# Convolution-branch layer norm: the reciprocal deviation computed with tokens on partitions and spread by diagonal products

## What is computed

```python
u_a = a_val * jax.nn.sigmoid(a_gate)
v_a, nb_a = _causal_dwconv(u_a, buf_a, conf_dw)          # width 31
v_a = v_a + conf_dw_b
y_a = silu(_layernorm(v_a, conf_ln_g, conf_ln_b)) @ conf_pw
# _layernorm: mu, var over the 512 channels of a token;
#   (x - mu) * rsqrt(var + EPS) * g + b
```

## Time and profile before

| | us |
|---|---|
| median of 3 runs | 876.55 |
| lowest, highest | 872.9, 877.35 |
| profiled execution, its time | 875.98 |
| profiled execution, its span | 874.2 |
| TensorE busy | 840.3 (96%) |
| VectorE busy | 683.9 (78%) |
| ScalarE busy | 465.0 (53%) |
| GpSimd busy | 74.3 (9%) |

### The profile page before, as it was taken

One profiled execution on the slowest core, in us unless ns is written; L12 is line 12 of the kernel. 1 busy time (PEld: TensorE's weight loads), 2 busy tenths in 40 slices (PEclk: granted clock), 3 DMA queues, 4 the chain that ended last, 5 costly groups with the idle time before them and its releaser, 6 DMA issues.

```text
span 874.2 us, 14904 instructions
## 1 busy us (share of the span) xinstructions
PE 840.3 (96%) x5047; PEld 698.9 (80%) x5047; DVE 683.9 (78%) x939; ACT 465.0 (53%) x556; POOL 74.3 (9%) x71
## 2 busy tenths in 40 slices
PE   7899999999999999999999989999999999999994
PEld 2489999989899999899777457888888888887841
DVE  0772637978797777599448889999899998999877
ACT  4642442343432221632222458888888888888741
POOL 0002000000000000230000010000000010005640
PEclk9999999999999999999999999999999999999988
DMA  9868534445544221123761579978997899999752
GB/s 332 276 191 289 189 118 160 129 161 169 168 127 122 91 79 49 55 78 119 238 246 73 187 280 397 399 282 333 352 368 249 316 400 400 400 397 400 294 195 98
DMA packets 90998, 201.24 MB, mean 230 GB/s; under 512 B 8793, under 2 KB 13401, under 8 KB 90919
## 3 DMA queue, kind: packets, MB, share of 16 engines
q1 hardware_dynamic: 78813, 165.25, 53.6%
q0 software_dynamic: 5136, 18.42, 6.0%
q10 hardware_dynamic: 7003, 16.95, 5.3%
HBM read 182.97 MB, written 18.35 MB: 230 GB/s over the span
## 4 chain that ended last, share of the span: by engine, by line
PE 84%; DVE 8%; ACT 2%; issue 2%; DMA 2%; ACTq 1%; SPq 1%; DVEq 0%
PE ps L802 31%; PE ps L653 13%; PE ps L655 13%; PE ps L654 13%; PE ps L882 3%; DVE w_lo L1587 2%; DMA region_a<-in_x_prompt_dram 2%; PE ps L997 2%; PE ps L834 2%; PE ps L1119 1%; ACT w_hi L1144 1%; PE ps L1123 1%; PE ps L681 1%; PE ps L682 1%; PE ps L1032 1%
## 5 line engine op out<-in xcount | busy, mean ns | idle before, releaser
L1587 DVE TENSOR_TENSOR w_lo<-raw,w_hi 128x1024 fp32r<-128x1024 f32 x202 | 241.4, 1225 | 100.1 <-ACT w_hi L1144 98.3
L1144 ACT ACTIVATE w_hi<-raw 128x1024 fp32r<-128x1024 f32 x202 | 207.8, 1056 | 197.5 <-PE ps L802 150.6
L653 PE MATMUL ps<-w_hi,hT_hi 128*128 128x512 f32 (+1 forms) x512 | 205.4, 401 | 3.0 <-DVE hT_lo L1587 1.8
L655 PE MATMUL ps<-w_hi,hT_lo 128*128 128x512 f32 (+1 forms) x512 | 202.1, 395 | 0.0
L654 PE MATMUL ps<-w_lo,hT_hi 128*128 128x512 f32 (+1 forms) x512 | 201.5, 394 | 0.0
L802 PE MATMUL ps<-hT_hi,w_hi 128*128 128x260 f32 x768 | 156.4, 285 | 3.5 <-DVE w_lo L1587 2.4
L802 PE MATMUL ps<-hT_lo,w_hi 128*128 128x260 f32 x768 | 155.0, 283 | 0.0
L802 PE MATMUL ps<-hT_hi,w_lo 128*128 128x260 f32 x768 | 154.9, 283 | 0.0
L802 PEld LDWEIGHTS ps<-hT_hi,w_hi 128*128 128x128 f32 x768 | 118.6, 189 | 6.6 <-DVE w_lo L1587 5.2
L802 PEld LDWEIGHTS ps<-hT_lo,w_hi 128*128 128x128 f32 x768 | 119.3, 190 | 0.0
L802 PEld LDWEIGHTS ps<-hT_hi,w_lo 128*128 128x128 f32 x768 | 118.9, 189 | 0.0
(11 more groups left out here) (328 smaller groups left out, 840.8 us busy)
## 6 DMA issues: line engine op xcount, KB each, us to landing
raw<-in_exp_w_dram SPq DMA_DIRECT2D x96, 512.0 KB
region_a<-in_exp_w_dram SPq DMA_DIRECT2D x80, 512.0 KB
raw<-in_w_in_dram SPq DMA_DIRECT2D x48, 512.0 KB
raw<-in_w_ada_dram SPq DMA_DIRECT2D x30, 512.0 KB
expert_rows<-region_b ACTq DMA_DIRECT2D x17, 512.0 KB, 6.5
region_b<-in_exp_w_dram SPq DMA_DIRECT2D x16, 512.0 KB
region_b<-in_w_ada_dram SPq DMA_DIRECT2D x14, 512.0 KB, 8.3
expert_rows<-region_a POOLq DMA_DIRECT2D x8, 512.0 KB, 8.7
```

The source lines that it names most:

```text
L653: pe.matmul(out, pairs[0], moving[0], start=start, stop=False)
L655: return pe.matmul(out, pairs[1], moving[0], start=False, stop=stop)
L1144: act.activation(w_hi[:, split_slot(n), :], place, ACT.Copy).then_inc(hi_done, 1)
L1587: return dve.tensor_tensor(out, whole, first.bitcast(F32), ALU.subtract)
```

## The change

Unit 11 no longer multiplies `ones_w` with the squares. Instead it makes, for each of five tiles of 128 tokens, four products with a chunk of the squares as the stationary side and one column of `ones_w` as the moving side: the mean square of each token, with tokens on partitions, in five columns of PSUM. The fifth tile takes the last 128 tokens, so it overlaps the fourth, and only its last 8 columns are used later. EPS, root, reciprocal and refinement run over 128 x 5; the last step also multiplies by 512. ScalarE scales the identity by each of the five columns (`rstd_diag`), TensorE multiplies `ones_w` with these five diagonals into the same PSUM set (`spread_rstd`, called ahead of t=2), and ScalarE copies the result to `rstdT` and frees the set. On VectorE, `merge(0)`, `lo(N_MIX+3)` and `merge(1)` now stand ahead of the four scalings of `va`.

```diff
--- before.py
+++ after.py
@@ -233,6 +233,9 @@
         sbr = carve(region_b, 10588, KW, NT)
         squares = carve(region_b, 0, KW, NT)
         rstdT = carve(region_b, 4280, NT)
+
+        rstd_diag = carve(region_b, 0, NTILE, P)
+        tok_first = (0, P, 2 * P, 3 * P, NT - P)
         tail = carve(region_b, 8500, 3, W)[0:40]
 
         h2 = [carve(region_b, at, D) for at in (0, 1024, 6144)]
@@ -328,6 +331,9 @@
         pads_ready = sem("pads_ready")
         conv_ready = sem("conv_ready")
         sq_ready = sem("sq_ready")
+        tok_rstd_ready = sem("tok_rstd_ready")
+        rstd_diag_ready = sem("rstd_diag_ready")
+        rstd_spread = sem("rstd_spread")
         centred = sem("centred")
         branch_b = sem("branch_b")
         branch_c = sem("branch_c")
@@ -862,11 +868,24 @@
                 product(next_set(), lambda k: w[:, g, (j % 2) * P:(j % 2 + 1) * P], lambda k: pooled[:, g, :], 1)
 
             pe.wait_ge(sq_ready, 1)
-            product(next_set(), lambda k: ones_w[:, :], lambda k: squares[:, k, :], KW)
-
+            rstd_set = next_set()
+            for i in range(NTILE):
+                for k in range(KW):
+                    mm = pe.matmul(ps[:, 2 * rstd_set, i:i + 1], squares[:, k, tok_first[i]:tok_first[i] + P], ones_w[:, 0:1], start=(k == 0), stop=(k == KW - 1))
+            mm.then_inc(mix_done, 1)
+
+            def spread_rstd():
+
+                pe.wait_ge(rstd_diag_ready, NTILE)
+                for i in range(NTILE):
+                    out, d = (ps[:, 2 * rstd_set, i * P:(i + 1) * P], rstd_diag[:, i, :]) if i < NP // P else (ps[:, 2 * rstd_set + 1, 0:ND], rstd_diag[:, i, P - ND:P])
+                    mm = pe.matmul(out, ones_w[:, :], d, start=True, stop=True)
+                mm.then_inc(rstd_spread, 1)
 
             for t in range(2 * KD):
                 n = N_MIX + 1 + t // 2
+                if t == 2:
+                    spread_rstd()
                 if t == 0:
                     pe.wait_ge(sbr_lo_done, KW)
                 if t % 2 == 0:
@@ -1278,7 +1297,13 @@
             for q in range(2, 5):
                 hi(N_MIX + q)
             act.wait_ge(ms_ready, 2)
-            act.activation(tmp_b[:, 0:NT], tmp_a[:, 0:NT], ACT.Sqrt).then_inc(root_ready, 1)
+            act.activation(sums[:, 2, 0:NTILE], sums[:, 1, 0:NTILE], ACT.Sqrt).then_inc(root_ready, 1)
+            act.wait_ge(tok_rstd_ready, 1)
+            for i in range(NTILE):
+                act.activation(rstd_diag[:, i, :], ident[:, :], ACT.Copy, scale=sums[:, 3, i:i + 1]).then_inc(rstd_diag_ready, 1)
+            act.wait_ge(rstd_spread, 1)
+            act.activation(rstdT[:, 0:NP], ps[:, 6, :], ACT.Copy)
+            act.activation(rstdT[:, NP:NT], ps[:, 7, 0:ND], ACT.Copy).then_inc(set_free[3], 1)
             for c in range(KW + 1):
 
                 if c < KW:
@@ -1833,12 +1858,16 @@
             lo(N_MIX + 1)
 
             s = unit(11)
-            link(dve.tensor_scalar(split(tmp_b[:, 0:NT]), halves(s), EPS, None, ALU.add), set_free[s], free_at(11))
-            dve.tensor_copy(tmp_a[:, 0:NT], tmp_b[:, 0:NT]).then_inc(ms_ready, 1)
-            dve.wait_ge(ms_ready, 2)
+            ms, root, out = (sums[:, r, 0:NTILE] for r in (1, 2, 3))
+            link(dve.tensor_scalar(ms, ps[:, 2 * s, 0:NTILE], EPS, None, ALU.add), ms_ready, 2)
             lo(N_MIX + 2)
-            lo(N_MIX + 3)
-            rsqrt(tmp_a[:, 0:NT], tmp_b[:, 0:NT], rstdT, tmp_b[:, 0:NT], 2)
+            dve.wait_ge(root_ready, 2)
+            link(dve.reciprocal(out, root))
+            link(dve.tensor_tensor(root, out, out, ALU.mult))
+            link(dve.tensor_tensor(root, root, ms, ALU.mult))
+            link(dve.tensor_scalar(root, root, -0.5, 1.5, ALU.mult, ALU.add))
+
+            dve.scalar_tensor_tensor(out, out, float(W), root, ALU.mult, ALU.mult).then_inc(tok_rstd_ready, 1)
 
             def merged_rest(p):
 
@@ -1855,9 +1884,11 @@
                 dve.tensor_tensor(gates[:, KD + j, :], gates[:, KD + j, :], tmp, ALU.add).then_inc(merged, 1)
 
 
+            merge(0)
+            lo(N_MIX + 3)
+            merge(1)
+            dve.wait_ge(set_free[3], free_at(11))
             for c in range(KW):
-                if c in (0, 3):
-                    merge(c // 3)
                 dve.tensor_tensor(va[:, c, :], va[:, c, :], rstdT, ALU.mult).then_inc(normed, 1)
             lo(N_MIX + 4)
             for t in range(2, 2 * KD):
```

## The result

The changed kernel takes 879.24 us (median of 19 runs, 875.85 to 881.86), the kernel before 875.07 (19 runs on the same footing, 872.74 to 877.51): a ratio of 1.0047, 95% interval 1.0035 to 1.0058. It is slower, by 3.1 to 5.1 us; the forecast was +0.4 us. The profiled execution took 880.76 us around a span of 879.0.

What follows compares the result with a forecast made beforehand. TensorE, busy 96% of the span, was taken as the bound. Sum of squares +0.93, spread +1.3 and removed pause -1.87 made +0.36 us on 875.98, so 876.3 us, with a range of 873.0 to 880.0.

Steps and rivals of the forecast that it cites:

- The small products: TensorE's sum of squares: 40 new instructions at 106 ns, 4.25 us, replace 3.32 us of removed products, +0.93 us.
- a row with equal weights: The router's product at 469.53 us, 128x128 FP32 weights under 20 columns, 106 ns per instruction, taken as the price.
- The spread: Five FP32 products with the diagonals on TensorE between t=1 and t=2: 10 instructions, +1.3 us.
- No wait for the diagonals: Diagonals ready at 373.8 us, TensorE asks at 375.1, so the wait before the spread costs 0.
- Rival B: Diagonals late because ScalarE loads a table before and after them; TensorE waits 1.3 us, 877.6 us; chance 0.08.
- The pause goes: TensorE's pause at unit t=6, from 385.8 to 387.67 us, disappears as merge(2) comes earlier on VectorE: -1.87 us.
- The sum without a fall: Terms added with the granted clock at 1.00 throughout: +0.93 + 1.3 - 1.87 = +0.36 us, 876.3 us; chance 0.48.
- rival A: TensorE's clock falls behind the new small products, losing 1.7 us: +2.1 us, 878.0 us; chance 0.28.
- the row at 468: Stretch from 468 to 472 us with 16 router products at granted clock 1.00, cited for a steady clock.
- the fall at 490: Stretch from 490 to 494 us after router products and 8x8 turns, mean clock 0.57, cited for a falling clock.
- A's longest fall: The longest clock fall in the profile before, 846 to 852 us, losing 3 us: 879.3 us if repeated here.
- a change below 0.5% was the likeliest: Whole-kernel outcome within 0.5% (4.4 us) of before given 0.88; faster 0.05, slower 0.07.

Runs made afterwards that it cites:

- run 2: The changed kernel with its 40 small-product instructions made 100 columns wide instead of one; stage 65.34 us, ratio to the kernel before 0.9993.
- Runs 7 and 10: The kernel before with only the new order on VectorE, all wide operations left, run twice; stage 63.25 us both times, ratios 0.9991 and 0.9984.
- 11: The changed kernel with small products 100 columns wide and `lo(N_MIX + 3)` back ahead of the root; stage 65.33 us, ratio to the kernel before 1.0009.
- runs 3 and 4: The kernel before plus 40 unused small-product instructions ahead of unit t=0, one column wide (stage 70.88 us, ratio 1.0059) or 100 columns (67.73 us, 1.0029).
- Run 1: The changed kernel measured again without any edit; stage 68.49 us, ratio to the kernel before 1.0037.
- run 12: The changed kernel measured a third time without any edit; stage 68.45 us, ratio to the kernel before 1.0027.
- run 5: The kernel before plus 40 unused one-column instructions, dealt out among the wide matmuls of unit t=0; stage 70.83 us, ratio 1.0088.
- run 6: The changed kernel with small products 100 columns wide and the last tile cut to its 8 tokens; stage 65.69 us, ratio to the kernel before 1.0013.

## Why the prediction was wrong

- **The small products**: 4.25 us forecast at 106 ns each, measured 4.39 at 110 (full clock). Right, and so is where the price came from, a row with equal weights. The Trainium skill's floor of about 25 ns (TensorE: Matmul & The Clock Gate, the section on the 56 ns gap) was rightly set aside: over four times as much is measured.
- **The spread**: 1.3 forecast, 1.04 measured; a small term that was 0.26 too high.
- **No wait for the diagonals**: right; run 2 has them at 375.1 and TensorE asks at 376.8. Rival B is out, though its table load stood where it was feared: 1.28 us ahead of the first Silu, hidden.
- **The pause goes**: right, -1.87. But its reason was only half of the matter: it was put down to VectorE's relief, and I followed the old queue to merge(2) and counted what was taken out of it, and did not price the new order by itself. Runs 7 and 10 show that the order alone is enough.
- **The sum without a fall**: +0.36 forecast; the runs with a steady clock (2, 11) give 65.34 and 65.33 against 65.20, +0.14.
- **The step that failed is the choice between the forecast and rival A.** A had the right mechanism, place and sign, and was given 0.28. The sum was made at a granted clock of 1.00 because the row at 468 kept it. But that row has 16 such instructions with matmuls of 512 columns before them, while the fall at 490 has only small ones just before it (router products and 8x8 turns, 487.32 to 490.70), and I wrote myself that the new products look most like the latter. A fall belonged in the sum: against the 65.34 of the steady clock it cost 1.5, 3.2 and 3.1 us in the three profiles, 2.6 on the mean, which makes the stage +2.7 over before. A's own price was 1.7 for a low stretch of 3.4 us. That fits the first profile; in the other two the stretch was 6.8 us, and only A's longest fall, priced at 3, comes near.
- The range held the median, 879.24, but only because it had been drawn wide enough for the long fall of A; the forecast itself, +0.4 us, was a tenth of the 4.2 measured. That a change below 0.5% was the likeliest held.
- The Trainium skill (TensorE: Matmul & The Clock Gate, the section on the clock gate) has the clock follow how busy the array is. The busy time in these rows, 4.00 of 4.00 us both at 1.00 and at 0.59, does not tell one from the other, so no row here confirms it; what does tell them apart are runs 3 and 4, one column against 100.

**What stays open.** The stage gives +2.7 us of the 3.1 to 5.1 measured. The expert loop adds 0.4: from the first turn of rows in it to the last 270.78 us before (534.39 to 805.17), and after 271.17. The two ends in the changed kernel, from its chain of waits:

```profile
540.25 0.87 PE ps L1016 x8
...
811.42 0.87 PE ps L1016 x8
```

All fourteen profiles have one of these two values, within 0.02: 270.77 where the loop began before 536 us and 271.17 where it began after 538, with the clock at full in both. What tells them apart was not found.

What the profiles leave over can be sought in the other executions, since each has its span and its mean granted clock on record. An estimate from these: span times clock is what would be left at full clock, the rest is lost to the low level. Run 1 gives 861.8 us against 861.5 for before in the same rounds, run 12 gives 861.0 against 861.1; no difference within an interval of 1.1 us. Lost to the low clock are 15.7 against 12.3 us, and 15.8 against 13.0. So the 3.7 and 2.8 us between these means go with the clock (3.4 and 2.8, each with an interval of 2.4 either way), and run 2, with 100 columns, is level in both (861.5 and 12.4 against 861.5 and 12.3). For the 19 executions of the first measurement the two numbers are 861.4 and 16.1; how much of this is a fall elsewhere than in the stage is open.

The clock falls in other places too, whatever the kernel: near 40 us in all fourteen profiles, between 490 and 532 in thirteen, and after 836 in all. Near 40 it is low for 13.6 us or a little more in five of the six profiles with the diagonals and in one of the other eight. Whether that is chance was not tested; run 2, which has it in its profile, lost no more to the clock than before on the mean of its executions.

## What to carry to other kernels

Count a small matmul on TensorE twice, at its start-to-start price and for what it does to the clock of those behind it; if more moving columns leave its price as it is (here 100 in place of one, 110 ns with both), give it more. When a change takes work out of a queue and also reorders it, price the order alone first: here it alone brought the whole gain, and the machinery that was built beside it only cost. A rival that the nearest row supports better than the forecast does belongs in the sum.

## What was not expected of the hardware

- 40 instructions of one-column FP32 products with weights of 128 columns were followed by a low granted clock for 3.4 or 6.8 us in five profiles of five, though TensorE never paused; also when each product stood behind a matmul of 260 columns (run 5: 0.50 over 377 to 381 us). In a row and with 100 columns they were not, in four of four, at the same 110 ns.
- 8 weight columns instead of 128 took nothing off an FP32 product of 100 moving columns (run 6: 4.42 us for 40, against 4.39).
- A VectorE operation with two SBUF operands took 1.6 to 2.6 times as long beside GpSimd (1.09 and 1.80 against 0.70 us, 2.34 against 1.22), and a reorder of VectorE's list that keeps most of its work clear of GpSimd's took 1.95 us off the stage.
